# Forgetting attention: transposes two tasks behind the scores in place of one, two buffers of probabilities, and selection columns read with step zero

## The chip, the cores and the metric

One core of one Trainium2 chip. The time is device time in microseconds (us) of one launch. The core has five engines with a queue each: TensorE (PE, with its weight loads as PEld), VectorE (DVE), ScalarE (ACT), GpSimd (POOL) and SyncE (SP, which issues DMAs here). An engine works its queue in the order written and stops at a wait on a semaphore.

## The reference

One layer of a streaming encoder on 512 tokens of width 1024, all in float32:

```
proj   = rms_norm(x) @ w_in                       # q, k, v, gates of both mixers
y_fox  = softmax(q k^T + c_i - c_j, causal) @ v   # forgetting attention, 8 heads of 64
y_ml   = mlstm(silu(conv(mq, mk)), mv, gates)     # 4 heads of 128, normalised by head, times a sigmoid
merged = g_fox * (y_fox @ w_up_fox) + g_ml * (y_ml @ w_up_mlstm)
h      = x + merged @ w_mix_out
h      = h + cross_attention(rms_norm(h), rms_norm(mem))      # 4 heads of 256, 256 memory tokens
h      = h + relu(rms_norm(h) @ w_mlp_in)^2 @ w_mlp_out
out    = rms_norm(h)
```

Here c is the running sum of the log forget gates. All vectors and weights are float32.

## The kernel before

Weight products keep float32 precision with three matmuls each: both factors are split into a high part (rounded to fp32r) and a low part (the rest), and high*high, high*low and low*high are summed. The weights come in slabs of 128 rows by 512 columns. SyncE loads four slabs at a time into one of two halves of `stage`; the step `split_weights` takes a pair of them: ScalarE copies the high parts into `w_hi` (L583), VectorE subtracts for the low parts in `w_lo` (L791). A ring of 12 slabs holds both.

The work of TensorE is a list of units (`fox_v`, `fox_q`, `fox_k`, `conv_q`, `conv_k`, `ml_v`, `ml_o`, `gate_fox0`, `gate_ml0`, `gate_fox1`, `up_fox0`, `up_ml0`, and so on to `mlp_out7`). A unit has mostly 4 groups (one PSUM bank each) and a group two halves of 12 matmuls of 512 columns (L1061); a group of an up unit is one half. The halves are numbered through the whole program and everything else is hung on these numbers: `make_steps` writes one list of steps, with `before(h, ...)` ahead of half h and `after(h, ...)` behind it. Each engine then walks the same list and emits its share of each step. The steps `split_weights` are placed by the halves that free their slots in the ring and the halves that need them, at the ends of units.

Forgetting attention goes in 16 tasks t: pairs of heads p = t // 4 by blocks of 128 query tokens i = t % 4, with 128 (i + 1) keys. Task t starts ahead of half `pair_at[t]` = 23 + 2t, so a task spans two halves. Its steps are:

- `pair_scores` (PE, L1125 and L1127): for both heads d of the pair the products q k in three parts and, as a fourth (`q == 3`), the decay. That one multiplies a selection column of `pick` (a 1 in the rows of one head, repeated in 128 columns) with the rows `decay`. Then the causal mask. It waits for both exponentials of the task before (`s_fexp`), which free the banks.
- `pair_exp`: VectorE takes the row maxima (`peak`, L926), ScalarE the exponentials into `prob` with their sums in `total` (L703). ScalarE waits there for the transposes of the task before, since `prob` is one buffer.
- `pair_norm` (DVE): reciprocal of the sums (L931), two multiplications of `prob` (L933).
- `pair_turn` (PE, L1137): transposes of `prob` into banks 4 and 5; waits for `pair_norm`.
- `pair_turned` (ACT, L583 `prob_t`): copy to SBUF.
- `pair_values` (PE, L1151): probabilities times `fox_v`.

In the units `conv_q` and `conv_k` every group brings more work: ScalarE copies the bank into `conv_u` and starts `conv_acc` (L620), VectorE adds three taps (L811), ScalarE takes the tanh, VectorE multiplies (`silu`, L860). `fox_split` splits the output of a pair of heads.

After the last fox task come 16 mLSTM tasks, one a half, at `place[t]`: scores (L1168 to L1170; `pick` again in L1169), maxima and stabiliser on VectorE (L948 to L952), `dwt` on ScalarE (L716), the weighted scores `prob` on VectorE (L959), transposes (L1195), the copy `prob_t` (L583), values (L1208). At the end of each head, in steps hung on `place`: `ml_quotient` (DVE, L971 to L978), `ml_squares` (L984, L985), `ml_norm` (13 short instructions, then L989), `ml_turn` (PE transposes, L1215), `ml_split` (L994 to L997). The unit `up_fox0` reads the fox output, `up_ml0` the mLSTM output; each of their groups ends with a VectorE instruction on `gate_f` or `gate_m` (L820, L826) that frees the bank.

GpSimd builds the constants at the start (`pick` in L542), loads small parameters, and later loads `h_tok` (the residual x), once the last `ml_norm` is done (L562).

Of the kernel before, what the change touches and what calls it, by code (L numbers as in the profile page):

```python
# [9 lines left out]
ALU = mybir.AluOpType  # L10
# [130 lines left out]
def make_steps():  # L141
# [4 lines left out]
    def before(h, *what):  # L146
        at.setdefault(h, ([], []))[0].extend(what)
# [23 lines left out]
    for t in range(N_FOX):  # L171
        before(pair_at[t] + 4, ("pair_values", t))
    for t in range(N_FOX):
        before(pair_at[t] + 2, ("pair_turn", t))
# [4 lines left out]
    for t in range(N_FOX):  # L179
        after(pair_at[t] + 2, ("pair_turned", t))  # L180
    place = [pair_at[-1] + 4 + t for t in range(X0)]
# [13 lines left out]
    for p in range(PAIRS):  # L195
        after(pair_at[NT * p + NT - 1] + 4, ("fox_split", p))
# [65 lines left out]
def trunk(nc, x, mem, norm_mix, norm_xattn, norm_mem, norm_mlp, w_in, b_fox_f, b_mlstm_i, b_mlstm_f,  # L262
# [6 lines left out]
    with ExitStack() as ctx:  # L269
# [14 lines left out]
        pick = sb("pick", [P, rows, P], F32R)  # L284
# [18 lines left out]
        total = sb("total", [P, 2])  # L303
        inv = sb("inv", [P, 2])
# [200 lines left out]
        def _(pool):  # L505
# [36 lines left out]
            fill(pool.tensor_copy(pick[:], pick_row[:].unsqueeze(2).to_broadcast([P, rows, P])))  # L542
# [38 lines left out]
        def _(act):  # L581
# [87 lines left out]
            for step, n in steps:  # L669
# [27 lines left out]
                elif step == "pair_exp":  # L697
                    keys = P * (n % NT + 1)
                    act.wait_ge(s_fpeak, n + 1)
                    if n >= 1:  # L700
                        act.wait_ge(s_fturn, n)
                    for d in range(2):
                        act.activation(prob[:, d, 0:keys], bank[2 + d][:, 0:keys], ACT.Exp,  # L703
                                       bias=peak[:, d:d + 1], accum_out=total[:, d:d + 1]).then_inc(s_fexp, 1)
# [56 lines left out]
        def _(dve):  # L761
# [113 lines left out]
            for step, n in steps:  # L875
# [52 lines left out]
                elif step == "pair_norm":  # L928
                    keys = P * (n % NT + 1)
                    dve.wait_ge(s_fexp, 2 * (n + 1))  # L930
                    link(dve.reciprocal(inv[:], total[:]))  # L931
                    for d in range(2):
                        dve.tensor_scalar(prob[:, d, 0:keys], prob[:, d, 0:keys], inv[:, d:d + 1], None, ALU.mult)\  # L933
                           .then_inc(s_fprob, 1)
# [9 lines left out]
                elif step == "probs":  # L944
# [10 lines left out]
                    if n >= 2:  # L955
                        dve.wait_ge(s_pturn, n - 1)
                    else:
                        dve.wait_ge(s_fturn, N_FOX)
# [52 lines left out]
        def _(pe):  # L1011
# [98 lines left out]
            def pair_scores(t):  # L1110
                p, i = t // NT, t % NT
                keys, tok = P * (i + 1), slice(P * i, P * i + P)
                cols = slice(decay_at(i), decay_at(i) + keys)
                if t == 0:
                    pe.wait_ge(s_dlow, NT + 1)
                if i == 0:
                    taken(pe, GROUP0[UNIT["fox_k"]] + p)
                if t >= 1:
                    pe.wait_ge(s_fexp, 2 * t)
                for q in range(4):  # L1120
                    for d in range(2):
                        r = slice(FOX_HD * d, FOX_HD * d + FOX_HD)
                        still = pick[r, 2 * p + d, :] if q == 3 else (fq_hi, fq_hi, fq_lo)[q][r, p, tok]
                        moving = decay[r, cols] if q == 3 else (fk_hi, fk_lo, fk_hi)[q][r, p, 0:keys]
                        pe.matmul(bank[2 + d][:, 0:keys], still, moving, start=(q == 0), stop=False)  # L1125
                for d in range(2):
                    ins = pe.matmul(bank[2 + d][:, P * i:keys], ident_b[:], hide_b[:], start=False, stop=True)  # L1127
                ins.then_inc(s_fscore, 1)

            def pair_turn(t):  # L1130
# [4 lines left out]
                for d in range(2):  # L1135
                    for j in range(i + 1):
                        ins = pe.transpose(bank[4 + d][:, P * j:P * j + P], prob[:, d, P * j:P * j + P], ident[:])  # L1137
# [18 lines left out]
            def scores(t):  # L1156
# [12 lines left out]
                pe.matmul(s[:, 0:keys], pick[0:64, FOX_HEADS + h, :], decay[0:64, cols], start=True, stop=False)  # L1169
# [133 lines left out]
```

## Time and profile before

| | |
|---|---|
| median of 3 runs | 1020.69 us (1017.74 to 1022.41) |
| the profiled execution | 1020.99 us, span 1019.3 us |
| busy: PE, PEld | 983.0 us (96%), 780.1 us (77%) |
| busy: DVE, ACT, POOL | 480.7 us (47%), 350.0 us (34%), 14.9 us (1%) |
| chain that ended last: PE, DVE, ACT | 84%, 10%, 4% |
| mean granted TensorE clock | 0.99 |

How to read it: the span is the time from the first to the last instruction in the trace, and the time of the execution holds some 1.7 us around it. Busy shares are means over stages. The chain that ended last is followed back from the last instruction to what released it each time. The granted clock is TensorE's, as a share of 2.4 GHz.

### The profile page before, as it was taken

The numbers are of one execution on the slowest core, as the hardware profiler recorded it, in microseconds if no ns is written. First come the engines' busy times: TensorE is split into PE (matmuls) and PEld (weight loads), VectorE is DVE, ScalarE is ACT, GpSimd is POOL, SyncE is SP. The second block draws the span as 40 slices with busy tenths as digits, with TensorE's granted clock in tenths as the row PEclk, the third lists the DMA queues.
The fourth block names the chain that finished last, engine by engine and source line by source line (L and its number), as shares of the span: only waits on it lengthen the run. The fifth ranks groups of instructions, "written<-read, shape, count | busy, mean of one in ns | idle before, by whom it ended". The sixth has DMA issues, their size and how long they took to land.

```text
span 1019.3 us, 11659 instructions
## 1 busy us (share of the span) xinstructions
PE 983.0 (96%) x4681; PEld 780.1 (77%) x4681; DVE 480.7 (47%) x873; ACT 350.0 (34%) x562; POOL 14.9 (1%) x37
## 2 busy tenths in 40 slices
PE   7999897999999999999999999999999999999996
PEld 6778675777777878889877668888888888888885
DVE  6632555533367653777234435643344334334435
ACT  4431553444334223245244422432134123213411
POOL 4000000000000000000000000000000000000000
PEclk8999999999999999999999999999999999999999
DMA  8311210221021352333422222222223322222212
GB/s 272 104 36 68 83 55 29 84 83 60 23 83 42 137 186 88 106 124 104 165 83 83 83 83 83 84 82 83 83 83 98 128 106 83 82 83 83 85 40 82
DMA packets 44205, 92.60 MB, mean 91 GB/s; under 512 B 1676, under 2 KB 1768, under 8 KB 44152
## 3 DMA queue, kind: packets, MB, share of 16 engines
q1 hardware_dynamic: 42584, 86.54, 25.5%
q0 software_dynamic: 1568, 5.32, 1.6%
q8 instruction: 37, 0.61, 0.2%
q14 instruction: 16, 0.13, 0.0%
HBM read 89.76 MB, written 2.10 MB: 90 GB/s over the span
## 4 chain that ended last, share of the span: by engine, by line
PE 84%; DVE 10%; ACT 4%; issue 2%; DMA 0%; ACTq 0%; DVEq 0%
PE bank L1061 74%; DVE w_lo L791 3%; DVE conv_acc L811 2%; PE bank L1230 1%; ACT w_hi L583 1%; PE bank L1125 1%; PE bank L1074 1%; PE bank L1181 1%; PE bank L1137 1%; PE bank L1168 1%; PE bank L1195 1%; PE bank L1208 1%; PE bank L1085 1%; ACT conv_acc L620 1%; PE bank L1151 1%
## 5 line engine op out<-in xcount | busy, mean ns | idle before, releaser
L1061 PE MATMUL bank<-act_hi,w_hi 128*128 128x512 f32 (+2 forms) x624 | 251.0, 402 | 2.3 <-DVE act_lo L887 2.3
L1061 PE MATMUL bank<-act_lo,w_hi 128*128 128x512 f32 (+2 forms) x624 | 246.0, 394 | 0.0
L1061 PE MATMUL bank<-act_hi,w_lo 128*128 128x512 f32 (+2 forms) x624 | 246.0, 394 | 0.0
L791 DVE TENSOR_TENSOR w_lo<-stage,w_hi 128x1024 fp32r<-128x1024 f32 x156 | 184.0, 1221 | 116.3 <-ACT w_hi L583 116.0
L583 ACT ACTIVATE w_hi<-stage 128x1024 fp32r<-128x1024 f32 x156 | 156.4, 1050 | 198.6 <-PE bank L1061 193.7
L1061 PE MATMUL bank<-w_hi,act_hi 128*128 128x512 f32 x448 | 179.3, 400 | 3.0 <-DVE act_lo L887 2.0
L1061 PE MATMUL bank<-w_hi,act_lo 128*128 128x512 f32 x448 | 178.2, 398 | 0.0
L1061 PE MATMUL bank<-w_lo,act_hi 128*128 128x512 f32 x448 | 178.0, 397 | 0.0
L1061 PEld LDWEIGHTS bank<-act_hi,w_hi 128*128 128x128 f32 x624 | 119.1, 191 | 28.2 <-issue 2.5
L1061 PEld LDWEIGHTS bank<-act_hi,w_lo 128*128 128x128 f32 x624 | 118.7, 190 | 27.3
L1061 PEld LDWEIGHTS bank<-act_lo,w_hi 128*128 128x128 f32 x624 | 119.0, 191 | 25.5
L1061 PEld LDWEIGHTS bank<-w_hi,act_hi 128*128 128x128 f32 x448 | 84.7, 189 | 24.3 <-DVE act_lo L887 2.5
L1061 PEld LDWEIGHTS bank<-w_lo,act_hi 128*128 128x128 f32 x448 | 84.7, 189 | 20.4 <-issue 0.2
L1061 PEld LDWEIGHTS bank<-w_hi,act_lo 128*128 128x128 f32 x448 | 84.7, 189 | 20.3
L844 DVE TENSOR_TENSOR h_tok<-bank,h_tok 128x512 f32<-128x512 f32 x48 | 33.1, 690 | 99.2 <-PE bank L1061 99.2
L850 DVE TENSOR_TENSOR relu<-relu 128x512 f32<-128x512 f32 x32 | 22.2, 692 | 69.3 <-ACT relu L644 69.3
L644 ACT ACTIVATE relu<-bank 128x512 f32<-128x512 f32 x32 | 19.2, 599 | 82.8 <-PE bank L1061 82.8
L703 ACT ACTIVATE prob<-bank,peak 128x128 f32<-128x128 f32 (+3 forms) x32 | 16.6, 524 | 51.5 <-DVE peak L926 51.5
L853 DVE TENSOR_TENSOR act_lo<-relu,act_hi 128x512 fp32r<-128x512 f32 x32 | 22.2, 693 | 22.3 <-ACT act_hi L583 22.3
L583 ACT ACTIVATE act_hi<-bank 128x512 fp32r<-128x512 f32 x32 | 17.7, 596 | 39.7 <-PE bank L1074 32.5
L583 ACT ACTIVATE act_hi<-relu 128x512 fp32r<-128x512 f32 x32 | 20.2, 632 | 24.3 <-DVE relu L850 24.3
L811 DVE SCALAR_TENSOR_TENSOR conv_acc<-conv_u,param,conv_acc 128x512 f32<-128x512 f32 x24 | 18.0, 752 | 21.9 <-ACT conv_acc L620 21.3
(215 smaller groups left out, 914.0 us busy)
## 6 DMA issues: line engine op xcount, KB each, us to landing
stage<-in_w_in SPq DMA_DIRECT2D x22, 1024.0 KB, 5.1
stage<-in_w_mlp_in SPq DMA_DIRECT2D x16, 1024.0 KB, 5.3
stage<-in_w_mlp_out SPq DMA_DIRECT2D x16, 1024.0 KB, 5.1
stage<-in_w_xkv SPq DMA_DIRECT2D x8, 1024.0 KB, 5.0
stage<-in_w_mix_out SPq DMA_DIRECT2D x4, 1024.0 KB, 5.1
stage<-in_w_xq SPq DMA_DIRECT2D x4, 1024.0 KB, 5.1
stage<-in_w_xo SPq DMA_DIRECT2D x4, 1024.0 KB, 5.1
x_tok<-in_x SPq DMA_DIRECT2D x4, 512.0 KB, 10.7
```

The source lines that it names most:

```text
L583: return act.activation(dst, src, ACT.Copy, **k)
L620: act.activation(conv_acc[:, c % 2, :], b[:], ACT.Identity, scale=conv_taps[:, c, 3:4], bias=conv_bias[:, c:c + 1]).then_inc(free, 1)
L644: act.activation(relu[:, a % 2, :], b[:], ACT.Relu).then_inc(free, 1)
L703: act.activation(prob[:, d, 0:keys], bank[2 + d][:, 0:keys], ACT.Exp, bias=peak[:, d:d + 1], accum_out=total[:, d:d + 1]).then_inc(s_fexp, 1)
L791: dve.tensor_tensor(w_lo[:, r:r + 2, :], src, w_hi[:, r:r + 2, :].bitcast(F32), ALU.subtract)\
L811: ins = dve.scalar_tensor_tensor(acc, u[:, q:q + TOK], conv_taps[:, c, q:q + 1], acc, ALU.mult, ALU.add)
L844: dve.tensor_tensor(dst, b[:], dst, ALU.add).then_inc(free, 1)
L850: dve.tensor_tensor(relu2[:, a % 2, :], relu[:, a % 2, :], relu[:, a % 2, :], ALU.mult)\
L853: dve.tensor_tensor(act2_lo[:, a % KT, :], relu2[:, a % 2, :], act2_hi[:, a % KT, :].bitcast(F32), ALU.subtract).then_inc(s_al, 1)
L1061: ins = pe.matmul(dst, still[q], moving[q], start=(k == 0 and q == 0), stop=(k == nk - 1 and q == 2))
L1074: ins = pe.transpose(bank[2 + 2 * (n % 2) + b][:, P * q:P * q + P], scaled[:, n % 2, P * k:P * k + P], ident[:])
L1085: ins = pe.matmul(bank[6][0:16, :], w[:, k, :], a[:, k, :], start=(k == 0 and q == 0), stop=(k == KT - 1 and q == 2))
```

## The change

The steps `pair_turn`, `pair_turned` and `pair_values` of forgetting attention move back by one task (two halves): the transposes of task t stand ahead of the scores of task t + 2. All that follows the fox tasks (`place`, and with it every mLSTM step) moves back by two halves; the halves and the weight splits stay. A second buffer `prob_b` takes the odd tasks, and `pair_total` has the sums for two tasks, so the exponentials of task t wait for the transposes of task t - 2. The wait of the first mLSTM tasks for the last fox transposes goes. `pick` holds one column per head, and the matmuls read it 128 times with step zero. The cost in SBUF is 4 KB more for `prob_b` and 6 KB less for `pick` in each partition.

```diff
     for t in range(N_FOX):
-        before(pair_at[t] + 4, ("pair_values", t))
+        before(pair_at[t] + 6, ("pair_values", t))
     for t in range(N_FOX):
-        before(pair_at[t] + 2, ("pair_turn", t))
+        before(pair_at[t] + 4, ("pair_turn", t))
...
     for t in range(N_FOX):
-        after(pair_at[t] + 2, ("pair_turned", t))
-    place = [pair_at[-1] + 4 + t for t in range(X0)]
+        after(pair_at[t] + 4, ("pair_turned", t))
+    place = [pair_at[-1] + 6 + t for t in range(X0)]
...
     for p in range(PAIRS):
-        after(pair_at[NT * p + NT - 1] + 4, ("fox_split", p))
+        after(pair_at[NT * p + NT - 1] + 6, ("fox_split", p))
...
-        pick = sb("pick", [P, rows, P], F32R)
+        pick = sb("pick", [P, rows], F32R)
...
+        pair_total = sb("pair_total", [P, 2, 2])
+        prob_b = sb("prob_b", [P, 2, TOK])
...
-            fill(pool.tensor_copy(pick[:], pick_row[:].unsqueeze(2).to_broadcast([P, rows, P])))
+            fill(pool.tensor_copy(pick[:], pick_row[:, 0:rows]))
...
-                    if n >= 1:
-                        act.wait_ge(s_fturn, n)
+                    if n >= 2:
+                        act.wait_ge(s_fturn, n - 1)
                     for d in range(2):
-                        act.activation(prob[:, d, 0:keys], bank[2 + d][:, 0:keys], ACT.Exp,
-                                       bias=peak[:, d:d + 1], accum_out=total[:, d:d + 1]).then_inc(s_fexp, 1)
+                        act.activation((prob, prob_b)[n % 2][:, d, 0:keys], bank[2 + d][:, 0:keys], ACT.Exp,
+                                       bias=peak[:, d:d + 1],
+                                       accum_out=pair_total[:, n % 2, d:d + 1]).then_inc(s_fexp, 1)
...
-                    link(dve.reciprocal(inv[:], total[:]))
+                    link(dve.reciprocal(inv[:], pair_total[:, n % 2]))
                     for d in range(2):
-                        dve.tensor_scalar(prob[:, d, 0:keys], prob[:, d, 0:keys], inv[:, d:d + 1], None, ALU.mult)\
-                           .then_inc(s_fprob, 1)
+                        p = (prob, prob_b)[n % 2][:, d, 0:keys]
+                        dve.tensor_scalar(p, p, inv[:, d:d + 1], None, ALU.mult).then_inc(s_fprob, 1)
...
                     if n >= 2:
                         dve.wait_ge(s_pturn, n - 1)
-                    else:
-                        dve.wait_ge(s_fturn, N_FOX)
...
-                        still = pick[r, 2 * p + d, :] if q == 3 else (fq_hi, fq_hi, fq_lo)[q][r, p, tok]
+                        still = pick[r, 2 * p + d:2 * p + d + 1].to_broadcast([FOX_HD, P]) if q == 3 else (fq_hi, fq_hi, fq_lo)[q][r, p, tok]
...
-                pe.matmul(s[:, 0:keys], pick[0:64, FOX_HEADS + h, :], decay[0:64, cols], start=True, stop=False)
+                pe.matmul(s[:, 0:keys], pick[0:64, FOX_HEADS + h:FOX_HEADS + h + 1].to_broadcast([64, P]), decay[0:64, cols], start=True, stop=False)
```

The order on TensorE ahead of half 33, between two halves (L1061, in the changed kernel L1062). `prob_t` are copied transposes, `ident,prob` are transposes, `fk_hi,fq_hi` the scores of task 5. Before:

```order
L1061 MATMUL bank<-act_hi,w_lo 128x512
L1151 MATMUL bank<-prob_t,fox_v 64x128 [waits s_fpt]
L1151 MATMUL bank<-prob_t,fox_v 64x128 x7
L1137 MATMUL bank<-ident,prob 128x128 [waits s_fpt,s_fprob]
L1137 MATMUL bank<-ident,prob 128x128
L1125 MATMUL bank<-fk_hi,fq_hi 128x256 [waits s_fexp]
```

And in the changed kernel:

```order
L1062 MATMUL bank<-act_hi,w_lo 128x512
L1153 MATMUL bank<-prob_t,fox_v 64x128 [waits s_fpt]
L1153 MATMUL bank<-prob_t,fox_v 64x128 x5
L1138 MATMUL bank<-ident,prob_b 128x128 [waits s_fpt,s_fprob]
L1138 MATMUL bank<-ident,prob_b 128x128 x7
L1126 MATMUL bank<-fk_hi,fq_hi 128x256 [waits s_fexp]
```

Ahead of the same scores stand the transposes of task 3 (8 of them, from `prob_b`) in place of those of task 4 (2), and the values of task 2 in place of those of task 3.

The order on VectorE where head 1 of mLSTM ends (heads count from 0): L978 is the last instruction of its quotient, L948 to L952 and L959 are the next task. Before:

```order
L978 TENSOR_TENSOR ml_h<-bank,ml_stat 128x512 [waits s_mturn,s_value,s_chain]
L948 TENSOR_REDUCE ml_m<-bank 128x1 [waits s_score]
L950 SCALAR_TENSOR_TENSOR ml_top<-ml_m,c_tile,c_all 128x1 [waits s_chain]
L952 TENSOR_TENSOR ml_m<-c_tile,ml_top 128x1 [waits s_chain]
L959 ISA prob,ml_den<-bank,dwt 128x128 [waits s_pturn,s_exp]
```

And in the changed kernel:

```order
L979 TENSOR_TENSOR ml_h<-bank,ml_stat 128x512 [waits s_mturn,s_value,s_chain]
L794 TENSOR_TENSOR w_lo<-stage,w_hi 128x1024 [waits s_high] x2
L951 TENSOR_REDUCE ml_m<-bank 128x1 [waits s_score]
L953 SCALAR_TENSOR_TENSOR ml_top<-ml_m,c_tile,c_all 128x1 [waits s_chain]
L955 TENSOR_TENSOR ml_m<-c_tile,ml_top 128x1 [waits s_chain]
L960 ISA prob,ml_den<-bank,dwt 128x128 [waits s_pturn,s_exp]
```

A weight split (two pairs of slabs, `x2`) now stands between them.

The order on VectorE at the end of head 3, from its quotient (L978) over the squares (L984, L985) to the norm (L784 and on). Before:

```order
L978 TENSOR_TENSOR ml_h<-bank,ml_stat 128x512 [waits s_mturn,s_value,s_chain]
L984 TENSOR_TENSOR ml_h_72<-ml_h 128x512 [waits s_yml,s_numer]
L985 TENSOR_REDUCE ml_stat<-ml_h_72 128x4 [waits s_chain]
L784 TENSOR_SCALAR ml_stat<-ml_stat 128x4 [waits s_chain]
L785 TENSOR_SCALAR ml_stat<-ml_stat 128x4 [waits s_chain]
```

And in the changed kernel:

```order
L979 TENSOR_TENSOR ml_h<-bank,ml_stat 128x512 [waits s_mturn,s_value,s_chain]
L794 TENSOR_TENSOR w_lo<-stage,w_hi 128x1024 [waits s_high] x2
L985 TENSOR_TENSOR ml_h_72<-ml_h 128x512 [waits s_yml,s_numer]
L986 TENSOR_REDUCE ml_stat<-ml_h_72 128x4 [waits s_chain]
L823 SCALAR_TENSOR_TENSOR gate_f<-gate_f,bank 128x512 [waits s_taken0,s_half,s_chain]
L787 TENSOR_SCALAR ml_stat<-ml_stat 128x4
```

A weight split stands ahead of the squares, and the first step of `up_fox0` (L823) between the squares and the norm.

## Rows read from the trace of the kernel before

**Rows 1.** The page: span, and busy time of TensorE.

```profile
span 1019.3 us, 11659 instructions
...
PE 983.0 (96%) x4681; PEld 780.1 (77%) x4681; DVE 480.7 (47%) x873; ACT 350.0 (34%) x562; POOL 14.9 (1%) x37
```

**Rows 2.** The waits of PE: total us, times, longest us.

```profile
PE bank L1137 <- DVE prob L933: 11.6, 10, 2.8
...
PE bank L1195 <- ACT prob_t L583: 1.0, 2, 0.7
...
PE bank L1061 <- DVE gate_f L820: 0.5, 1, 0.5
```

**Rows 3.** One fox task in order of time: start, us, instruction, count, idle before.

```profile
134.36 2.33 DVE L811 SCALAR_TENSOR_TENSOR conv_acc<-conv_u,param,conv_acc 128x512 f32<-128x512 f32 x3 [2.77 <-ACT conv_acc L620]
...
136.79 0.88 DVE L933 TENSOR_SCALAR prob<-prob,inv 128x512 f32<-128x512 f32 x2
...
133.53 0.80 ACT L620 ACTIVATE conv_acc<-bank,param 128x512 f32<-128x512 f32 x1
...
135.32 0.88 PE L1151 MATMUL bank<-prob_t,fox_v 128*64 128x128 f32 x12
137.73 0.87 PE L1137 MATMUL bank<-ident,prob 128*128 128x128 f32 x6 [1.53 <-DVE prob L933]
```

**Rows 4.** The same, PE, at a task without a wait.

```profile
210.84 0.88 PE L1151 MATMUL bank<-prob_t,fox_v 128*64 128x128 f32 x12
211.64 1.09 PE L1137 MATMUL bank<-ident,prob 128*128 128x128 f32 x8
```

**Rows 5.** Window (PE busy, clock, DMA), and two half starts, in order of time.

```profile
160.00:170.00 10.00, 8.82 (x48) 0.91 0.00 0
...
158.94 0.78 PE L1061 MATMUL bank<-act_hi,w_hi 128*128 128x512 f32 x1
...
163.12 0.40 PE L1061 MATMUL bank<-act_hi,w_hi 128*128 128x512 f32 x1
```

**Rows 6.** End of mLSTM head 3, in order of time, DVE and PE.

```profile
343.28 0.69 DVE L984 TENSOR_TENSOR ml_h<-ml_h 128x512 f32<-128x512 f32 x1
...
344.73 0.17 DVE L784 TENSOR_SCALAR ml_stat<-ml_stat 128x4 f32<-128x4 f32 x1
...
347.32 0.69 DVE L989 TENSOR_TENSOR ml_h<-ml_h,ml_stat 128x512 f32<-128x512 f32 x1
349.39 2.36 DVE L791 TENSOR_TENSOR w_lo<-stage,w_hi 128x1024 fp32r<-128x1024 f32 x2 [1.38 <-ACT w_hi L583]
...
348.04 0.39 PE L1061 MATMUL bank<-act_hi,w_hi 128*128 128x512 f32 x1
...
350.85 0.60 PE L1215 MATMUL bank<-ident,ml_h 128*128 128x128 f32 x4
```

**Rows 7.** Window of the fox stage: busy PE, PEld, DVE, ACT, POOL, clock, DMA.

```profile
110.00:150.00 40.00, 35.38 (x215) 26.87 (x215) 23.27 (x37) 18.25 (x37) 0.00 (x0) 1.00 0.19 63
```

**Rows 8.** mLSTM head 1, in order of time, DVE, ACT and PE.

```profile
309.54 0.28 DVE L948 TENSOR_REDUCE ml_m<-bank 128x1 f32<-128x128 f32 x1
...
310.56 0.48 ACT L583 ACTIVATE prob_t<-bank 128x384 f32<-128x384 f32 x1
...
311.53 0.60 PE L1195 MATMUL bank<-ident,prob 128*128 128x128 f32 x4
...
321.88 0.27 ACT L583 ACTIVATE prob_t<-bank 128x128 f32<-128x128 f32 x1
...
322.30 0.41 PE L1195 MATMUL bank<-ident,prob 128*128 128x128 f32 x2 [0.69 <-ACT prob_t L583]
```

**Rows 9.** The load of h_tok (order of time), and its first use.

```profile
348.58 0.75 POOL L562 DMA_DIRECT2D h_tok<-in_x  x1 [335.82 <-DVE ml_h L989]
...
L844 DVE TENSOR_TENSOR h_tok<-bank,h_tok x48: 680/692/692, 425.4 to 1010.8; 128x512 f32<-128x512 f32 x48
```

**Rows 10.** Weight loads of pick: ns min/median/max, first and last start us.

```profile
L1125 PEld LDWEIGHTS bank<-decay,pick x32: 184/185/188, 103.0 to 236.8; 64*128 64x128 f32 x32
```

More of the change, by code:

```diff
@@ L1136, in pair_turn @@
                     for j in range(i + 1):
-                        ins = pe.transpose(bank[4 + d][:, P * j:P * j + P], prob[:, d, P * j:P * j + P], ident[:])
+                        ins = pe.transpose(bank[4 + d][:, P * j:P * j + P], (prob, prob_b)[t % 2][:, d, P * j:P * j + P],
+                                           ident[:])
                 ins.then_inc(s_fturn, 1)
```

## The prediction

> **What bounds the kernel now.** I read the page first: TensorE is busy 983.0 us of a span of 1019.3 us [rows 1], so a change can win only what lies in its 36 us of idle time, or in a slow clock. The second view is the list of waits of TensorE [rows 2]: its longest entry is the transposes of the probabilities (line 1137), which waited 10 times, 11.6 us in all, for the normalisation on VectorE (line 933). The two short entries there belong to the mLSTM tasks and to up_fox, and come back below.
>
> The third view is one task of forgetting attention in order of time [rows 3]. VectorE takes its queue in order. The normalisation of a task stands in it behind three convolution steps (2.33 us), and these wait for the ScalarE instruction conv_acc, which needs a group of matmuls that ends in the middle of the task. So conv_acc starts at 133.53, the three steps at 134.36, and the normalisation ends at 136.79 + 0.88 = 137.67. TensorE had finished its two halves and came to the values at 135.32. It starts the transposes at 137.73, after 1.53 us of idle time. Nothing else of that task is late. The same pair of steps without a wait stands in [rows 4]: values at 210.84, transposes at 211.64, thus 0.80 us apart in place of 2.41. The loss is 1.61 us where the listed wait is 1.53: each wait costs 0.07 us beyond its entry.
>
> The fourth view is the clock [rows 5]. After the longest wait (2.8 us, in the sixth task) the granted clock of 160 to 170 us is 0.91, and the half that starts at 158.94 ends at 163.12: 4.18 us, where a half takes 2.81 us at full clock (348.04 to 350.85 [rows 6]) and 2.89 us when a block of small matmuls stands ahead of it. That half ran partly at the lower of the two levels, 1.2 GHz in place of 2.4. The wait thus cost 1.3 us more there, and 0.2 us in the matmuls just ahead.
>
> **Part 1: transposes two tasks behind the scores.** The dependence stays, but TensorE asks for it a whole task later. A task is two halves (5.8 us) and some 2 us of small matmuls. The normalisation was late by at most 2.8 us, so all ten waits end before TensorE comes. Recovered: 11.6 + 10 x 0.07 + 1.5 = **13.8 us**. The copy of the transposes and the values move back with them, and nobody but the next values waits for them.
>
> What is late next? The scores of a task wait for the exponentials of the one before. VectorE is busy 23.27 of 40 us, ScalarE 18.25 of 40 [rows 7], so both keep up on average. Where weights are split, two pairs of slabs cost VectorE 2.36 us of a task (the row at 349.39 [rows 6]). With reduction, silu, convolution, normalisation and such a split, VectorE has some 7.6 us of work in a task that shrinks to about 8 us, so it recovers a lag slowly. By hand, with the durations of these rows, the exponentials come within 2 us of the next scores in the sixth task and just in time in the tenth. I take **0.2 us** of new waits; the bounds are 0 and 3 us (three split places at 1 us).
>
> **Part 2: everything of mLSTM two halves later.** The place where the weights are split does not move, since it follows the halves. So the order on VectorE changes, and two splits now stand ahead of steps that TensorE waits for.
>
> Head 1. Before, VectorE goes from line 978 straight to the reduction at 309.54; ScalarE copies prob_t at 310.56 to 311.04, and the transposes start at 311.53 without a wait [rows 8]. Now a split stands ahead of that reduction: +2.36 us, less 0.09 of overlap. The copy ends at 313.31, and the transposes start 0.14 us behind it, as they do at 322.30 behind a copy that ends at 322.15. That is 313.45 in place of 311.53: a new wait of **1.9 us**. The next split delays the task behind as it did, so the 0.69 us wait at 322.30 stays.
>
> Head 3. Count from the start of half 78, with turn-over at 2.89, 5.70, 8.52 and 11.33. The split starts 1.35 us behind the end of the half that it waits for (349.39 against 348.04): 4.24 to 6.6. It now stands ahead of the squares. These and the norm take 4.73 us before (343.28 to 347.32 + 0.69 [rows 6]), and the norm, from 344.73, begins 1.45 us into them and lasts 3.28 us. Between them now stands an up_fox step (0.69 us), which waits for the half that ends at 8.52. So squares end at 8.0, that step at 9.4, the norm at 12.7. TensorE wants the transposes of head 3 at 11.33: a new wait of **1.4 us**. In exchange the 0.5 us wait of the up_fox half for gate_f [rows 2] goes (0.6 with its restart), since the last step of head 3 no longer stands ahead of it.
>
> Head 0. The split that delayed its tasks (the smaller of the two waits for prob_t, 1.0 us together [rows 2]) moves ahead of another task, where the same sum gives about 0.5 us. Net zero.
>
> Together the shift costs 1.9 + 1.4 - 0.6 = **2.7 us**. The bounds are 0 (if the ScalarE copies get ahead) and 6 us (if each of the five splits in the stage costs a whole 1.2 us).
>
> The load of h_tok on GpSimd's queue is issued two halves later too, since it waits for the norm of head 3: before at 348.58, first used at 425.4 [rows 9]. A shift of 7 us against 77 us costs nothing.
>
> **Part 3: selection columns with step zero.** 32 + 16 weight loads read one element 128 times in place of 128 neighbours. No row of before has such a load. The nearest is the same load with unit step: 184 to 188 ns [rows 10], run beside matmuls. I take **0**. The upper bound is a doubling, all of it exposed: 48 x 0.185 = 8.9 us. Below it is 0 as well: a quicker load lies under a matmul and gains nothing.
>
> The Trainium skill (TensorE: Matmul & The Clock Gate, section "LDWEIGHTS (loading the stationary operand)") says that a load takes its number of columns at 1.2 GHz, estimated at 107 ns for 128, whatever lies in the rows; by that rule step zero leaves the load as it is. The trace agrees only in part: the measured 185 ns is not 107. Another page of the Trainium skill (SBUF — State Buffer, section "Door 1: The DMA port swizzle", on 16-byte lines) has reads slow down when each crosses to a new line, and step zero never does; by that the term is zero or below.
>
> **Part 4: rest.** The copy into pick on GpSimd shrinks from 1536 to 12 columns at the start, where the first transposes wait for the first norm and not for it: 0. The wait of the first two mLSTM tasks for the last fox transposes goes: 0, it was long fulfilled. The second buffer of probabilities and the smaller pick move the addresses of the buffers behind them by some 2 KB: 0.
>
> **Sum.** The profiled execution took 1020.99 us (span 1019.3), 0.3 us above the median of the three runs. 1020.99 - 13.8 + 0.2 + 2.7 = 1010.1 us; against the median 1009.8. I forecast **1010 us**.
>
> **Rivals.**
> 1. The mLSTM shift is free: its waits are absorbed and 13.8 us is all gain, 1020.7 - 13.8 = 1006.9 us. For it: one split delays a step that has time elsewhere in the stage. Against: a split of before already shows as the 0.69 us wait. Chance 0.12.
> 2. The wait moves to the scores. VectorE and ScalarE fall behind in the convolution stage and half of the 13.8 us comes back as waits for the exponentials: 1009.8 + 6.9 = 1016.7 us. For it: the hand count has the tenth task just in time. Against: half of the ten waits lie in tasks without a split, and VectorE is busy 58% of the stage. Chance 0.12. That the change does not do what it says belongs here: were the transposes still late, they would be late by a part of a task.
> 3. Slower: the step-zero load is a different thing to the hardware, is not pulled ahead, and costs on the path. It decides from (10.9 + 5.1) / 48 = 0.33 us a load for slower by over 0.5%; at 0.4 us it gives 1009.8 + 19.2 = 1029 us. For it: no row shows one. Against: the same number of elements leaves the same number of cycles, and 0.33 us is more than a whole load of now. Chance 0.03.
> 4. The forecast: 0.73.
>
> **Numbers.** A measurement of this kernel tells a difference of some 0.5% (5.1 us) from none, so faster means below 1015.6 us. The three runs of before spread from 1017.7 to 1022.4. The range starts at 1006, below rival 1 by 1 us of that spread, and reaches 1016.5, which takes the 3 us of new fox waits, the 6 us bound of mLSTM and most of rival 2. Faster: forecast and rival 1, less what the bounds take above 1015.6, plus a part of rival 2: 0.86. Same: 0.11. Slower: 0.03.
>
> **What would show it.** The waits of TensorE for the normalisation gone from the list; the granted clock at 1.0 all through 150 to 170 us; new waits of the mLSTM transposes for prob_t of 1.5 to 2 us at head 1 and of the head-3 transposes for ml_h of about 1.4 us; the loads of pick at 182 to 190 ns. The prediction is wrong if waits of line 1126 for the exponentials appear beyond 1 us in all, if the pick loads leave that band, or if the stage from 98 to 250 us shrinks by less than 12 us.

## The result and the profile after

The changed kernel takes 991.44 us (median of 4 runs, 991.32 to 993.06), the kernel before 1019.99 us (4 runs, 1017.74 to 1022.41): a ratio of 0.9723, 95% interval 0.9705 to 0.974. The forecast was 1010.0 us with a range from 1006.0 to 1016.5. The sign was right, but 28.5 us were won where 10.7 were forecast (from 1020.7, the median known then), and the time lies below the range. The profiled execution took 991.38 us.

The page of the changed kernel, beside [rows 1]: TensorE's busy time fell by 25.0 us (983.0 to 958.0), though it runs the same 4681 matmuls. The forecast had counted only idle time, of which there were 36 us, and 1.5 us of slow clock. The last row here is one of the six groups of big matmuls; the page of before has it as the second fence shows, with a mean of 400 ns for one in place of 395.

```profile
span 989.6 us, 11656 instructions
...
PE 958.0 (97%) x4681; PEld 776.8 (78%) x4681; DVE 478.6 (48%) x873; ACT 349.6 (35%) x562; POOL 13.7 (1%) x37
...
L1062 PE MATMUL bank<-w_hi,act_hi 128*128 128x512 f32 x448 | 176.8, 395 | 5.1 <-DVE act_lo L890 3.5
```

```profile
L1061 PE MATMUL bank<-w_hi,act_hi 128*128 128x512 f32 x448 | 179.3, 400 | 3.0 <-DVE act_lo L887 2.0
```

The waits of TensorE (total us, times, longest us), beside [rows 2]. The ten waits of the transposes for the normalisation are gone, and so is the one for gate_f. No line here is of the scores (1126). New are waits of the values (1153) for prob_t, a larger wait of the mLSTM transposes (1197) for prob_t, and one of the head transposes (1217) for ml_h.

```profile
PE bank L1062 <- DVE act_lo L890: 5.9, 3, 2.4
PE bank L1153 <- ACT prob_t L585: 3.5, 3, 1.8
PE bank L1197 <- ACT prob_t L585: 3.3, 3, 1.8
PE bank L1197 <- DVE x_prob L946: 3.1, 4, 1.3
...
PE bank L1217 <- DVE ml_h L990: 1.3, 1, 1.3
```

The window that held the slow clock (columns as in [rows 7]). The granted clock is 1.00 in place of the 0.91 of [rows 5].

```profile
160.00:170.00 10.00, 9.53 (x59) 7.26 (x60) 6.51 (x10) 5.79 (x12) 0.00 (x0) 1.00 0.09 18
```

The wait at head 1 of mLSTM in order of time, beside [rows 8]. The split (L794) stands between the quotient (L979) and the reduction (L951), the copy of prob_t comes behind them, and the transposes start 0.15 us behind its end.

```profile
299.70 0.69 DVE L979 TENSOR_TENSOR ml_h<-bank,ml_stat 128x512 f32<-128x512 f32 x1
300.31 2.35 DVE L794 TENSOR_TENSOR w_lo<-stage,w_hi 128x1024 fp32r<-128x1024 f32 x2
...
302.58 0.28 DVE L951 TENSOR_REDUCE ml_m<-bank 128x1 f32<-128x128 f32 x1
...
303.61 0.48 ACT L585 ACTIVATE prob_t<-bank 128x384 f32<-128x384 f32 x1
...
304.24 0.63 PE L1197 MATMUL bank<-ident,prob 128*128 128x128 f32 x4 [1.82 <-ACT prob_t L585]
```

The other waits of these transposes and of the head transposes (L1217), in order of time: one in head 0, one two tasks behind that of head 1, and the one at head 3.

```profile
264.10 0.63 PE L1197 MATMUL bank<-ident,prob 128*128 128x128 f32 x4 [0.69 <-ACT prob_t L585]
...
315.03 0.41 PE L1197 MATMUL bank<-ident,prob 128*128 128x128 f32 x2 [0.81 <-ACT prob_t L585]
...
344.63 0.55 PE L1217 MATMUL bank<-ident,ml_h 128*128 128x128 f32 x3 [1.31 <-DVE ml_h L990]
```

The longest new wait of forgetting attention, in order of time. A split holds VectorE until 177.2, the reduction for the exponentials (L929) follows it, and ScalarE takes its queue in order: the exponentials (L705) first, then the copy of prob_t (L585), whose transposes had been done since 171.7. TensorE's values (L1153) wait for that copy.

```profile
174.89 2.36 DVE L794 TENSOR_TENSOR w_lo<-stage,w_hi 128x1024 fp32r<-128x1024 f32 x2 [1.06 <-ACT w_hi L585]
...
177.17 0.68 DVE L929 TENSOR_REDUCE peak<-bank 128x2 f32<-128x512 f32 x1
...
177.88 0.47 ACT L705 ACTIVATE prob_b<-bank,peak 128x256 f32<-128x256 f32 x1 [2.08 <-DVE peak L929]
...
178.79 1.02 ACT L585 ACTIVATE prob_t<-bank 128x1024 f32<-128x1024 f32 x1
...
179.87 1.09 PE L1153 MATMUL bank<-prob_t,fox_v 128*64 128x128 f32 x16 [1.80 <-ACT prob_t L585]
```

The weight loads of pick, beside [rows 10], with step zero now: no change.

```profile
L1126 PEld LDWEIGHTS bank<-decay,pick x32: 184/185/188, 101.2 to 221.3; 64*128 64x128 f32 x32
```

The prediction named three signs of being wrong, and none showed: no wait of the scores, the loads of pick in their band, and the stage from the half that starts at 99.8 us before to the one at 252.4 us shrank from 152.6 to 138.1 us, by more than 12. All three watch the moved steps.

None of this accounts for 18 us. They show in stretches where nothing waits. The first fence is TensorE near 700 us of the kernel before (start, us, instruction), the second the same of the changed kernel. From start to start it is some 0.233 us before and 0.227 us after. The names are moving operand, then stationary operand.

```profile
699.76 0.40 PE L1061 MATMUL bank<-w_hi,act_lo 128*128 128x512 f32 x1
699.99 0.39 PE L1061 MATMUL bank<-w_hi,act_hi 128*128 128x512 f32 x1
700.22 0.39 PE L1061 MATMUL bank<-w_lo,act_hi 128*128 128x512 f32 x1
...
701.16 0.40 PE L1061 MATMUL bank<-w_hi,act_lo 128*128 128x512 f32 x1
```

```profile
699.73 0.39 PE L1062 MATMUL bank<-w_lo,act_hi 128*128 128x512 f32 x1
699.95 0.39 PE L1062 MATMUL bank<-w_hi,act_lo 128*128 128x512 f32 x1
700.18 0.39 PE L1062 MATMUL bank<-w_hi,act_hi 128*128 128x512 f32 x1
...
701.09 0.39 PE L1062 MATMUL bank<-w_lo,act_hi 128*128 128x512 f32 x1
```

Six spacings are 1.40 us before and 1.36 us after. The closer spacing is there already between 40 and 90 us, ahead of the first moved step (227.1 ns against 234.1), and the granted clock is 1.00 there and near 700 us in both. What the change does everywhere is to move buffers. The buffers lie one behind the other in SBUF: the rings of weights first (w_hi at byte 32,896 of a partition, w_lo 24,576 behind it), then small tiles with pick and prob_b among them, then a block at a0 whose activations all stand at whole multiples of 256 bytes from a0. The change moves a0 from 97,312 to 95,360. From w_hi to a0 it was 64,416 bytes, which is 160 modulo 256, and is 62,464, which is 0 modulo 256.

### The profile page after: what moved, and what is told of

Its sections match the earlier page's. It is cut to its first block, busy times and chain, and to the rows that moved or that the text cites. A ratio compares the mean times of both kernels' runs of the same rounds, so it can differ in the third digit from the quotient of the medians.

```text
span 989.6 us, 11656 instructions
## 1 busy us (share of the span) xinstructions
PE 958.0 (97%) x4681; PEld 776.8 (78%) x4681; DVE 478.6 (48%) x873; ACT 349.6 (35%) x562; POOL 13.7 (1%) x37
## 4 chain that ended last, share of the span: by engine, by line
PE 86%; DVE 8%; ACT 3%; issue 1%; DMA 1%; SPq 0%; ACTq 0%; DVEq 0%
PE bank L1062 75%; DVE w_lo L794 3%; PE bank L1232 1%; DVE conv_acc L814 1%; PE bank L1075 1%; PE bank L1183 1%; PE bank L1126 1%; PE bank L1170 1%; ACT w_hi L585 1%; DMA stage<-in_w_in 1%; PE bank L1153 1%; PE bank L1197 1%; PE bank L1138 1%; PE bank L1210 1%; PE bank L1086 1%
## 5 line engine op out<-in xcount | busy, mean ns | idle before, releaser
L1062 PE MATMUL bank<-act_hi,w_hi 128*128 128x512 f32 (+2 forms) x624 | 246.2, 395 | 2.4 <-DVE act_lo L890 2.4
L1062 PE MATMUL bank<-act_hi,w_lo 128*128 128x512 f32 (+2 forms) x624 | 241.1, 386 | 0.0
L1062 PE MATMUL bank<-act_lo,w_hi 128*128 128x512 f32 (+2 forms) x624 | 240.9, 386 | 0.0
L794 DVE TENSOR_TENSOR w_lo<-stage,w_hi 128x1024 fp32r<-128x1024 f32 x156 | 183.9, 1220 | 112.6 <-ACT w_hi L585 112.4
L585 ACT ACTIVATE w_hi<-stage 128x1024 fp32r<-128x1024 f32 x156 | 156.4, 1051 | 187.1 <-PE bank L1062 179.8
L1062 PE MATMUL bank<-w_hi,act_hi 128*128 128x512 f32 x448 | 176.8, 395 | 5.1 <-DVE act_lo L890 3.5
L1062 PE MATMUL bank<-w_lo,act_hi 128*128 128x512 f32 x448 | 175.1, 391 | 0.0
L1062 PE MATMUL bank<-w_hi,act_lo 128*128 128x512 f32 x448 | 175.0, 391 | 0.0
L1062 PEld LDWEIGHTS bank<-act_hi,w_hi 128*128 128x128 f32 x624 | 117.8, 189 | 24.7 <-issue 2.6
L1062 PEld LDWEIGHTS bank<-act_hi,w_lo 128*128 128x128 f32 x624 | 117.7, 189 | 23.8
L1062 PEld LDWEIGHTS bank<-act_lo,w_hi 128*128 128x128 f32 x624 | 117.9, 189 | 22.0
L1062 PEld LDWEIGHTS bank<-w_hi,act_hi 128*128 128x128 f32 x448 | 84.4, 188 | 23.6 <-DVE act_lo L890 4.0
L1062 PEld LDWEIGHTS bank<-w_hi,act_lo 128*128 128x128 f32 x448 | 84.5, 189 | 17.7
L1062 PEld LDWEIGHTS bank<-w_lo,act_hi 128*128 128x128 f32 x448 | 84.6, 189 | 17.2 <-issue 0.2
L646 ACT ACTIVATE relu<-bank 128x512 f32<-128x512 f32 x32 | 19.2, 599 | 77.9 <-PE bank L1062 77.9
L585 ACT ACTIVATE act_hi<-bank 128x512 fp32r<-128x512 f32 x32 | 17.7, 596 | 37.2 <-PE bank L1075 30.0
L585 ACT ACTIVATE act_hi<-relu 128x512 fp32r<-128x512 f32 x32 | 20.2, 633 | 24.8 <-DVE relu L853 24.8
L719 ACT ACTIVATE dwt<-bank,ml_m 128x128 f32<-128x128 f32 (+3 forms) x16 | 8.4, 528 | 45.2 <-DVE ml_m L955 45.2
```

Of the source, the lines that this page charges most:

```text
L585: return act.activation(dst, src, ACT.Copy, **k)
L646: act.activation(relu[:, a % 2, :], b[:], ACT.Relu).then_inc(free, 1)
L794: dve.tensor_tensor(w_lo[:, r:r + 2, :], src, w_hi[:, r:r + 2, :].bitcast(F32), ALU.subtract)\
L1062: ins = pe.matmul(dst, still[q], moving[q], start=(k == 0 and q == 0), stop=(k == nk - 1 and q == 2))
```

## The experiments

Every ratio is to runs of the kernel before made beside that kernel on the same chip; their medians lie between 1019.39 and 1021.15 us, so a ratio is not the quotient of two times in this table. "Spacing" is the mean from start to start of neighbouring big matmuls (line 1061 of before) from 40 us on, some 3,190 pairs with gaps between 210 and 250 ns, first those that move weights, then those that move activations. "Distance" is a0 less w_hi, modulo 256 bytes.

| kernel | order | distance | spacing, ns | us | ratio |
|---|---|---|---|---|---|
| before | before | 160 | 233.4 / 234.2 | 1019.99 | 1 |
| e3_step0_alone | before | 160 | 233.4 / 234.2 | 1020.56 | 1.0002 |
| e1_before_pad32 | before | 192 | 230.5 / 233.3 | 1013.60 | 0.9929 |
| e4_before_pad64 | before | 224 | 233.3 / 233.3 | 1019.42 | 0.9984 |
| e5_before_pad96 | before | 0 | 227.1 / 227.4 | 1000.65 | 0.9823 |
| after | after | 0 | 227.1 / 227.4 | 991.44 | 0.9723 |
| e2_after_pad32 | after | 32 | 233.3 / 233.3 | 1009.78 | 0.9895 |
| e6_after_pad64 | after | 64 | 233.3 / 230.2 | 1005.25 | 0.9856 |
| e8_after_ring64 | after | 64 | 233.3 / 230.1 | 1005.99 | 0.9867 |
| e7_after_pad128 | after | 128 | 233.1 / 232.9 | 1007.93 | 0.9884 |
| e9_after_both64 | after | 0 | 227.1 / 227.4 | 991.53 | 0.9720 |
| e10_after_pad256 | after | 0 | 227.1 / 227.4 | 993.11 | 0.9733 |

**A pad of 32 bytes.** The changed kernel, and the kernel before, each with 32 unused bytes ahead of a0; no instruction differs but for its addresses.

```diff
+        pad = sb("pad", [P, 8])
         a0 = nc.sbuf_base
```

> The changed kernel with 32 bytes of padding ahead of the activation buffers, which puts their base 32 past a multiple of 64 (95392), as in the kernel before. Theory A: the spacing of the big matmuls goes back to 234 ns and the time to what the order alone gives, 1010 us by my sum plus the 3.5 us of waits of the fox values that I did not have, 1010 to 1016. Theory B: 991 us as without the padding.

Measured: 1009.78 us, ratio 0.9895 (0.9879 to 0.9911), at the lower end of what theory A had for it. The pad alone costs 18.3 us (17.5 by the two ratios): the step from 233.3 back to 227.1 and 227.4 ns over 1,322 and 1,866 pairs is 19.2 us, and the waits behind prob_t shrink by 1.2 us at the wider spacing (2.5 and 3.1 us in place of 3.5 and 3.3). So addresses are 18 us of the result, and what is left of the change is what had been forecast for it as a whole.

> The kernel before with 32 bytes of padding ahead of the activation buffers, which puts their base at a multiple of 64 bytes (97344) in place of 32 past one (97312); no step moves. Theory A (the base of the buffers sets how fast the big matmuls follow each other: 227 ns apart in the trace after, 234 before): 3696 matmuls by 7 ns, 26 us at most, less what waits give back: 995 to 1000 us, spacing 227. Theory B (the spacing comes from the new order or from step zero): 1020 us, spacing 234. My recorded sum (10.9 us from the order) leaves this at 1020.

Measured: 1013.60 us, 0.9929 (0.9916 to 0.9943), thus 0.7% faster for a pad. Theory A in the form of this run, that a base at a multiple of 64 bytes gives full speed, is out: it had forecast 995 to 1000 us and 227 ns. The kernel before was itself at a bad distance, and 192 is a little less bad.

**Step zero alone.** The kernel before with the small pick, and an unused tile in the place of what it saves, so that no other address moves.

```diff
-        pick = sb("pick", [P, rows, P], F32R)
+        pick = sb("pick", [P, rows], F32R)
+        pick_pad = sb("pick_pad", [P, 1516])
```

> The kernel before with the selection columns read with step zero and nothing else: the freed space is padded so that every later buffer keeps its address. If step zero costs nothing: 1020 us and loads of pick at 184 to 188 ns. If step zero is what made the big matmuls faster (a rival to theory A): below 1000 us.

Measured: 1020.56 us, 1.0002 (0.9992 to 1.0012). Reading with step zero costs and gains nothing.

**Which distance.** The kernel before with pads of 64 and 96 bytes, the changed kernel with 64 and 128.

> The kernel before with 64 bytes of padding: base 97376, again 32 past a multiple of 64. Theory A with a period of 64 bytes: 1020 us and 234 ns, no change. If instead any shift of the buffers away from 97312 helps (a clash with some other buffer): 995 to 1000 us.

> The kernel before with 96 bytes of padding: base of the activation buffers 97408, a multiple of 128 (97312 is 32 past one; 97344 of the 32-byte run is 64 past one and had matmuls 231 to 233 ns apart, 1013.6 us). Theory A2 (full speed needs a base at a multiple of 128 bytes): spacing 227 ns, 996 to 1002 us. Theory A3 (the base matters only together with the new layout of the small buffers, or full speed needs some other residue): 1013 us or more.

> The changed kernel with 64 bytes of padding: base 95424, 64 past a multiple of 128. Theory A2: as the kernel before with 32 bytes of padding, spacing 231 ns where the activations are stationary and 233 where they move, 1002 to 1007 us. A3 leaves it open; a period of 64 bytes would leave 991 us.

> The changed kernel with 128 bytes of padding: base 95488, a multiple of 256, where 95360 is 128 past one. A2: 991 us and 227 ns, unchanged. A period of 256 bytes: back to 1007 to 1010 us.

Measured: 1019.42 us (0.9984, 0.9973 to 0.9996), 1000.65 us (0.9823, 0.9796 to 0.985), 1005.25 us (0.9856, 0.983 to 0.9882) and 1007.93 us (0.9884, 0.9853 to 0.9914). The kernel before with 96 bytes is at distance 0 and has the spacing of the changed kernel; its ten waits for the normalisation are still there, as its list of waits shows:

```profile
PE bank L1138 <- DVE prob L934: 12.9, 10, 3.0
```

So the two effects add up, as far as the noise tells: 1019.39 - 1000.65 = 18.7 us for addresses in the old order (15.3 to 20.8 by the interval), 18.3 us in the new one, and 1000.65 - 991.44 = 9.2 us for the order at distance 0 (10.2 by the two ratios). Part of the gain by addresses goes back into waits: the ten waits for the normalisation are 12.9 us here and 11.6 before, since TensorE comes to them sooner.

Theory A2, full speed at every multiple of 128 bytes, forecast e5 and falls with e7, where the period of 256 bytes holds. In e6 it has the time, but not the spacings: it had the matmuls with stationary activations at 231 ns and the others at 233, and they have 233.3 and 230.2. At 64 bytes only the matmuls that move activations gain, at 192 chiefly those that move weights. The cost is no single step away from zero.

**Distance or position.** First the rings of weights moved by 64 bytes and a0 by 128 (distance 64 again); then both by 64 (distance 0, each now 64 off its old place); then a0 by 256.

```diff
         stage = sb("stage", [P, STAGES, LOT, HALF_W])
+        pad_w = sb("pad_w", [P, 16])
         w_hi = sb("w_hi", [P, RING, HALF_W], F32R)
```

> The changed kernel with 64 bytes of padding ahead of the ring of split weights and 64 more ahead of the activations: weights at 32960 (64 past a multiple of 128), activations at 95488 (a multiple of 128). If only the activations' base matters: 991 us, 227 ns. If every operand of a matmul has to start at a multiple of 128 bytes: 231 to 233 ns, 1002 to 1010 us.

> The changed kernel with 64 bytes of padding ahead of the ring of split weights only: weights at 32960, activations at 95424, both 192 past a multiple of 256, so their distance stays 62464, a multiple of 256. Theory A4 (the distance between stationary and moving operand modulo 256 decides, since distances of 64 gave the same 229 and 233 ns in two kernels with different bases): 227 ns, 991 us. Theory A5 (each operand has to start 128 past a multiple of 256): 229 to 233 ns, 1003 to 1008 us.

> The changed kernel with 256 bytes of padding ahead of the activations only: base 95616, 128 past a multiple of 256 as 95360 is, distance 62720, a multiple of 256 but not of 512. A4 and A5 both: 227 ns, 991 us. A period of 512 bytes or more: 229 to 238 ns and 1003 us or more.

Measured: 1005.99 us (0.9867, 0.9841 to 0.9893), 991.53 us (0.9720, 0.9696 to 0.9744) and 993.11 us (0.9733, 0.9711 to 0.9756). The first equals e6 in time and spacing, the second and third equal the changed kernel. What counts is the distance between weights and activations modulo 256 bytes, and not where either stands. In e9 `stage` kept its place while weights, small tiles and activations moved together, so their distance from `stage` does not count either. Theory A5, a fixed residue for each operand, is out.

**Which two reads.** The low parts of the weights alone 32 bytes off, all else at distance 0.

```diff
+        pad_w = sb("pad_w", [P, 8])
         w_lo = sb("w_lo", [P, RING, HALF_W], F32R)
...
+        pad = sb("pad", [P, 56])
         a0 = nc.sbuf_base
```

> Changed kernel with 32 bytes between the high and the low parts of the weights and 224 bytes behind them: high parts and activations keep their distance (0 modulo 256), the low parts of the weights alone stand 32 bytes off. It asks which two reads disturb one another. Let the three matmuls of a k-slab with the weights stationary be A (w_hi, act_hi), B (w_hi, act_lo), C (w_lo, act_hi). Theory S (the matmul's own stationary operand against its moving operand): C alone stretches, to 231-234 ns from start to start, A and B stay at 226.7. Theory L (the weight load of the next matmul, which runs beside this one's moving operand): B stretches, since w_lo is loaded beside it, A and C stay. With the activations stationary both say the same: the matmul that moves w_lo stretches, the other two stay at 226.7. Time by either: a third of the 18 us, thus about 997 us. If any address off the grid slows all three, about 1010.

Measured: 1009.05 us, 0.9879 (0.9858 to 0.99), as if all were off. Both theories fall in their sizes. With the stationary operand named first, the mean spacings with weights stationary are 232.7 ns for (w_hi, act_hi), 237.8 for (w_hi, act_lo), beside which w_lo is loaded, and 228.9 for (w_lo, act_hi); the sum of 699.4 is three times 233.1. The load of the next weights beside this moving operand fits the largest of the three, but the first, with nothing off its grid, is slow as well. With activations stationary they are 232.5 ns for (act_hi, w_hi), 231.2 for (act_lo, w_hi) and 235.7 for (act_hi, w_lo), which moves w_lo: again the forecast one is the slowest, and the other two do not stay at 226.7. The time is that of the third case named above, that all three slow down. One operand in three off is enough for the whole price, and which reads collide stays open.

**The mLSTM shift alone.** The kernel before with `place` at + 6.

```diff
-    place = [pair_at[-1] + 4 + t for t in range(X0)]
+    place = [pair_at[-1] + 6 + t for t in range(X0)]
```

> The kernel before with all mLSTM steps two halves later and nothing else moved. The prediction's part 2: 2.7 us slower than before (1022.5 to 1024), with new waits of the mLSTM transposes for prob_t at head 1 of 1.9 us and of the head-3 transposes for ml_h of 1.4 us, and the wait for gate_f gone. Rival: the shift is free, 1020 us.

Measured: 1023.81 us, 1.0038 (1.0024 to 1.0051), thus 3.9 us slower, 2.4 to 5.2 by the interval, around the forecast 2.7. Its list of waits has the new ones of the forecast, with the old ten:

```profile
PE bank L1137 <- DVE prob L933: 11.6, 10, 2.8
...
PE bank L1195 <- ACT prob_t L583: 3.1, 3, 1.8
...
PE bank L1215 <- DVE ml_h L989: 1.2, 1, 1.2
```

From the start of half 24 to that of half 300 the trace has 884.71 us against 881.92 before: 2.8 us. The rest arises ahead of half 8, where this execution waited longer for the first split weights (3.2 us for w_lo, against 1.0). Rival 1, a free shift, is out.

**Splits behind the urgent steps.** If the shift costs because splits now stand ahead of steps that TensorE waits for, and the values wait because the copy stands behind the exponentials, both can be cured in the order. The changed kernel with the copy ahead of the exponentials, and with the splits behind all urgent steps of a half:

```diff
+    for t in range(N_FOX):
+        after(pair_at[t] + 4, ("pair_turned", t))
     for t in range(N_FOX):
         before(pair_at[t], ("pair_scores", t))
...
-    for t in range(N_FOX):
-        after(pair_at[t] + 4, ("pair_turned", t))
...
-        steps += [("split_weights", p) for p in pairs.get(i, []) if p % 4 >= 2]
         soon = [x for x in a if x[0] in ("pair_exp", "pair_norm", "pair_turned", "probs", "turned", "conv_tanh",
-                                      "conv_silu", "split_weights")]
+                                      "conv_silu", "split_weights", "ml_squares", "ml_norm")]
         steps += soon
+        steps += [("split_weights", p) for p in pairs.get(i, []) if p % 4 >= 2]
```

> The changed kernel with another order of steps at the same halves: the copies of the fox transposes ahead of the exponentials, and the splits of weights at the end of a unit behind the attention steps, squares and norms, in place of ahead of them. If the 3.5 us of waits of the fox values, the 3.3 us of the mLSTM transposes and the 1.3 us of the head-3 transposes come from steps that queue behind the splits: most of 8 us goes, 984 to 987 us. If the split then comes late for the halves (waits for w_lo), less or nothing: 991 us.

Measured: 982.83 us (981.27 to 982.95), 0.963 (0.9607 to 0.9653): 8.6 us below the changed kernel and a little better than the 984 to 987 that were forecast. In its list of waits the values and ml_h are gone (gate_f had gone before), prob_t of the mLSTM transposes is down to 2.0 us and x_prob, in cross attention, from 3.1 to 0.2 us:

```profile
PE bank L1197 <- ACT prob_t L585: 2.0, 2, 1.8
PE bank L1062 <- DVE w_lo L794: 1.7, 1, 1.7
...
PE bank L1197 <- DVE x_prob L946: 0.2, 1, 0.2
```

Here 3.5 + 1.3 + 1.3 + 2.9 = 9.0 us of waits have gone. The run changed three things together (the copies ahead of the exponentials, the splits last, squares and norms among the urgent steps) and does not tell how much each gave by itself.

The longer of the two waits that are left is still a split's doing. The split stands behind the steps of its own half, but ahead of the reduction (L951) of the next one:

```profile
305.90 2.35 DVE L794 TENSOR_TENSOR w_lo<-stage,w_hi 128x1024 fp32r<-128x1024 f32 x2
308.17 0.55 DVE L951 TENSOR_REDUCE ml_m<-bank 128x1 f32<-128x384 f32 x1
...
310.10 0.41 PE L1197 MATMUL bank<-ident,prob 128*128 128x128 f32 x2 [1.78 <-ACT prob_t L585]
```

**The place of mLSTM again, with the splits out of the way.** `place` at + 5 and at + 4 in that version.

> The changed kernel with the splits behind the urgent steps, and mLSTM one half later than before in place of two. Theory that the splits were what made the shift of mLSTM cost: within 1.5 us of the version with the splits last (982.8), since nothing is left that the place of mLSTM moves into. Rival, that the place itself costs (fox values and mLSTM tasks in one half are bunched): 1.5 to 3 us faster.

> The same with mLSTM where it stood before the change: the first mLSTM scores now stand ahead of the last fox values. By the first theory again within 1.5 us of 982.8; a new wait in the first mLSTM task (its exponentials queue behind those of the last fox task) could add about 1 us. Rival as above: 1.5 to 3 us faster.

Measured: 984.20 us (0.9646, 0.9623 to 0.9668) and 983.43 us (0.9624, 0.9599 to 0.965), within 1.4 us of 982.83. Single runs of the three versions reach from 981.2 to 987.0 us, so a cost of 1 us could hide here; one of 2.8 us for the two halves, as in the old order of the splits, does not show in the medians of + 4 and + 6 (983.43 and 982.83). The traces agree: the waits that follow the place are 2.0 us at + 6 (prob_t), 3.2 us at + 5 (0.8 prob_t, 1.3 gate_m, 1.1 at L1210 without a releaser in the profile) and 2.3 us at + 4 (0.5 prob_t, 0.6 gate_f, 1.2 at the first mLSTM scores, L1170, again without one). The place moves the waits about and hardly changes their sum.

## Why the prediction failed

**The failed step** is Part 4: "The second buffer of probabilities and the smaller pick move the addresses of the buffers behind them by some 2 KB: 0." The 1,952 bytes bring activations and weights to distance 0. By the spacings the gain against the kernel before is 1,324 x 6.3 + 1,859 x 6.8 ns = 21.0 us; with the pads, of which one starts from distance 32 and the other gives 1.3 us back in the ten waits, it measures 18.3 and 18.7 us. With this step fell the first sentence of the prediction, that a change can win only what lies in the 36 us of idle time or in a slow clock: TensorE's busy time shrank by 25.0 us. Nothing in the trace of before could give the size of this term: it shows one spacing and nothing to hold it against. But zero was taken without a bound, although the term touches the busy 983 us, and the others, but for 1.5 us of slow clock, only the idle 36. A bound could have been had from the big matmuls: one per cent of their spacing is some 7 us (3,190 x 0.233 us x 0.01).

**Part 1, the transposes** was right: all ten waits went and the clock stayed full. **The new waits of forgetting attention** were taken as 0.2 us with bounds 0 and 3; they are 3.5 us (2.5 at the wider spacing of e2). The cause was that of rival 2, VectorE held by splits, but the place was not: the scores never waited, since the exponentials stand first on ScalarE, and the values did, because their copy stands behind. The sentence "nobody but the next values waits for them" named the one who waits and gave it no price. As a wait of the scores rival 2 did not come true.

**Part 2, the mLSTM shift** was right: 1.82 us at head 1 where 1.9 stood, 1.3 at head 3 where 1.4 stood, the wait for gate_f gone, 2.8 us in the stretch of e11 against 2.7. The cause stands in the rows at 300.31 and 304.24, where the split holds the queue, and e12, e15 and e16 bear it out within the spread of their runs. The 0.69 us wait behind it, forecast to stay, is 0.81 us (the row at 315.03), and that of head 0, forecast at about 0.5 in place of some 0.3, is 0.69 us (the row at 264.10).

**Part 3, step zero** was right: 185 ns a load as before, and e3 measures 1.0002. The rule of the Trainium skill (TensorE: Matmul & The Clock Gate, section "LDWEIGHTS (loading the stationary operand)") that only the number of columns counts held for the step, while its 107 ns did not. Rival 3 is out.

With the sizes measured the sum closes to about 1 us: 1020.99 - 13.8 + 3.7 + 2.7 - 21.0 = 992.6 us, against 991.38 of the profiled execution (3.7 is 3.5 and three restarts at 0.07, a price that the prediction read from one wait). For the order alone at the old kind of distance, -13.8 + 2.6 + 2.7 = -8.5 us; e2 lies 1020.88 - 1009.78 = 11.1 us below the runs beside it (9.1 to 12.4 by the interval), of which 1.7 is spacing (1,866 x 0.9 ns), thus -9.4, which agrees within the noise. That e2 lands on the forecast 1010 us is in part two errors that cancel, the waits of the values and this bit of spacing.

## What to carry to other kernels

Where TensorE is busy nearly all the time, an edit that adds, drops or resizes a buffer can be worth more than the order it was made for: compare the start-to-start spacing of the main matmul in a stretch without waits before reading anything else, and hold the addresses with a pad when a single edit is to be judged. Try a few pads of 32 bytes early; here a pad of 96 bytes alone took 1.8% off the kernel before. When a consumer is moved back, price the next instruction in the same queue too: the late one was the copy behind the exponentials, and moving that copy ahead, together with putting the splits, long work without a near deadline, behind the short urgent steps of a half, gave 8.6 us more.

## What was not expected of the hardware

The spacing of these 128x512 matmuls depends on the distance between the addresses of their operands modulo 256 bytes: 227.1 and 227.4 ns at 0, between 230.1 and 234.2 ns at 32, 64, 128, 160, 192 and 224 bytes. Moving both operands by 64 bytes changes nothing (e9), and neither does a distance that is a multiple of 256 and not of 512 (e10, 62,720 bytes). At the 2.4 GHz of the full granted clock the 226.7 ns of the stretch from 640 us on are 544 cycles for 512 columns, and the 233.3 ns of e2 are 560. Why 256 bytes, no run tells.

The Trainium skill (TensorE: Matmul & The Clock Gate, section "Back-to-back issue gap") gives N / 2.4 + 2.5 ns for isolated matmuls, estimated at 216 ns for 512 columns, and for a stream of weight loads and matmuls some 131 ns; the mean spacings here reach neither, at no distance. Another page of the Trainium skill (SBUF — State Buffer, section "Operand start alignment") says of its rule on start addresses that it is about legality, not speed. In this kernel every address was legal, and the difference was in speed alone.

One thing more: one third of the matmuls at a bad distance cost as much as all of them (e13). No run here tells which reads disturb each other: the two operands of one matmul, or the next weight load and the current moving operand.
